# Decode-token recurrence of a hybrid decoder layer: outputs from the old states in the value stage, new states beside the FFN's second products

## What is computed

```python
z = einsum('bld,dn->bln', rmsnorm(h), w_in)          # queries, keys, values, gates, merge gates
# per head, per token:  S_t = diag(a_t) S_{t-1} + k_t^T v_t ;  o_t = q_t S_t
o_h, s_h = _gated_recurrence(q_h, k_h, i_h, log_f, s_h0)     # 8 heads, 128 x 128
o_g, s_g = _gated_recurrence(q_g, k_g, v_g, log_a, s_g0)     # 4 heads, 128 x 256
y = (rmsnorm(o) * silu(gate)) @ w_up                  # each branch
merged = sigmoid(m_h) * y_h + sigmoid(m_g) * y_g
h = h + rmsnorm(merged @ w_out)
u = square(relu(rmsnorm(h) @ w_ff1)); h = h + rmsnorm(u @ w_ff2)      # D_FF = 8192
h = h + sigmoid(h @ w_ple_gate) * (p @ w_ple)
```

## Time and profile before

| | |
|---|---|
| timed runs, median | 1670.41 us |
| profiled execution, first to last instruction | 1668.5 us |
| TensorE busy | 1661.8 us (100%) |
| VectorE busy | 1094.9 us (66%) |
| ScalarE busy | 810.8 us (49%) |
| GpSimd busy | 201.4 us (12%) |
| DMA, mean | 191 GB/s |

### The profile page before, as it was taken

The page is one execution under the profiler, slowest core; times in us unless marked ns, Lnnn a source line. Parts: engine busy times, 40 slices in busy tenths (PEclk is TensorE's granted clock), DMA queues, the critical chain, the costliest instruction groups (busy, mean ns, idle before and its releaser), DMA issues.

```text
span 1668.5 us, 36779 instructions
## 1 busy us (share of the span) xinstructions
PE 1661.8 (100%) x13676; PEld 1657.1 (99%) x13676; DVE 1094.9 (66%) x1841; ACT 810.8 (49%) x1104; POOL 201.4 (12%) x196
## 2 busy tenths in 40 slices
PE   9999999999999999999999999999999999999999
PEld 9999999999999999999999999999999999999999
DVE  7558548989988987665697445554455445555774
ACT  8574435465465556543565334443345334443452
POOL 4100001211211100025320000000000000025200
PEclk9999999999999999999999999999999999999999
DMA  9555656665665567775555555555555555555564
GB/s 277 165 187 178 221 188 204 184 210 179 199 213 186 185 216 230 228 258 176 165 183 180 186 185 170 183 185 182 171 182 181 188 180 172 182 196 176 169 192 145
DMA packets 162596, 318.73 MB, mean 191 GB/s; under 512 B 11732, under 2 KB 96468, under 8 KB 162548
## 3 DMA queue, kind: packets, MB, share of 16 engines
q1 hardware_dynamic: 160244, 315.94, 59.4%
q10 hardware_dynamic: 2304, 2.16, 0.4%
HBM read 299.97 MB, written 18.09 MB: 191 GB/s over the span
## 4 chain that ended last, share of the span: by engine, by line
PE 99%; DVE 0%; issue 0%; ACT 0%; POOL 0%; POOLq 0%
PE bank L320 28%; PE bank L321 28%; PE bank L322 28%; PE bank L338 3%; PE bank L340 3%; PE bank L343 3%; PE bank L640 2%; PE bank L653 1%; PE bank L629 1%; PE bank L671 0%; PE bank L685 0%; PE bank L679 0%; PE bank L590 0%; PE bank L651 0%; PE bank L672 0%; PE bank L610 0%
## 5 line engine op out<-in xcount | busy, mean ns | idle before, releaser
L295 ACT CAST whi<-raw 128x1024 fp32r<-128x1024 f32 x533 | 548.5, 1049 | 495.8 <-PE bank L322 392.7
L320 PE MATMUL bank<-a_hi,whi 128*128 128x264 f32 x2576 | 737.1, 286 | 0.0
L321 PE MATMUL bank<-a_lo,whi 128*128 128x264 f32 x2576 | 729.9, 283 | 0.0
L322 PE MATMUL bank<-a_hi,wlo 128*128 128x264 f32 x2576 | 729.7, 283 | 0.0
L300 DVE TENSOR_TENSOR wlo<-raw,whi 128x1024 fp32r<-128x1024 f32 x518 | 628.3, 1244 | 128.6 <-ACT whi L295 128.1
L320 PEld LDWEIGHTS bank<-a_hi,whi 128*128 128x128 f32 x2576 | 485.4, 188 | 0.5 <-issue 0.3
L321 PEld LDWEIGHTS bank<-a_lo,whi 128*128 128x128 f32 x2576 | 485.6, 189 | 0.1
L322 PEld LDWEIGHTS bank<-a_hi,wlo 128*128 128x128 f32 x2576 | 483.2, 188 | 0.0
L320 PE MATMUL bank<-b_hi,whi 128*128 128x264 f32 x1280 | 363.2, 284 | 0.0
L321 PE MATMUL bank<-b_lo,whi 128*128 128x264 f32 x1280 | 362.6, 283 | 0.0
L322 PE MATMUL bank<-b_hi,wlo 128*128 128x264 f32 x1280 | 362.4, 283 | 0.0
(11 more groups left out here) (186 smaller groups left out, 1558.1 us busy)
## 6 DMA issues: line engine op xcount, KB each, us to landing
raw<-in_stream SPq DMA_DIRECT2D x533, 512.0 KB, 4.5
m_spill<-stage SPq DMA_DIRECT2D x32, 132.0 KB, 5.1
lev<-m_spill SPq DMA_DIRECT2D x16, 264.0 KB, 3.3
S<-in_state_hgrn SPq DMA_DIRECT2D x16, 256.0 KB, 5.3
out_new_hgrn_sample<-S SPq DMA_DIRECT2D x16, 256.0 KB, 4.6
S<-in_state_gla SPq DMA_DIRECT2D x8, 512.0 KB, 8.1
out_new_gla_sample<-S SPq DMA_DIRECT2D x8, 512.0 KB, 5.5
room<-in_x SPq DMA_DIRECT2D x7, 528.0 KB, 7.7
```

Source lines behind the costliest of these rows:

```text
L295: act.copy(whi[:, s, :], raw[:, s, :]).then_inc(hi_ready, 1)
L320: pe.matmul(out, whi[:, s, w], hi[:, k0 + k, :], start=start and k == 0, stop=False)
L321: pe.matmul(out, whi[:, s, w], lo[:, k0 + k, :], start=False, stop=False)
L322: mm = pe.matmul(out, wlo[:, s, w], hi[:, k0 + k, :], start=False, stop=stop and k == HT - 1)
```

## The change

The samples leave the heads.

- **Outputs from old states.** The output is computed as (q a) S + (q k) v, with q, a, k of the sample. During the value stage SyncE loads the old states in another layout: a *unit* is one head, 16 chunks of 8 key rows by 8 samples on the partitions, 8 key rows by the value width on the free dimension (128 x 1024 for HGRN, 128 x 2048 for GLA), in a ring of four. ScalarE scales a unit by eight ACTIVATEs with a per-partition scale (`SCALED_AT`: after the spill of value tiles 1 to 8, and 9, 11, 13, 14), VectorE sums it over the 8 key rows with one reduction (`SUMMED_AT`, a tile or two later), TensorE sums over the chunks with a product with `own_sample` of width 8 (`sample_out`: HGRN after value tile 11, GLA in head 0). The factors are transposed on TensorE, stored to DRAM and loaded back in the unit's layout in eight DMAs of 32-byte runs (`load_columns`), on ScalarE's queue for q a, on SyncE's for k and a.
- **Head 0** has the rest for all heads: own products, sum of squares, roots, norm (`whole_samples`, `sum_samples`, `sample_roots`, `normed_samples`). The other heads take their columns from `so_normed`.
- **New states.** 16 units of 128 x 1024 (a GLA head is two) in a ring of three, one every three second tiles of the FFN's first three blocks: VectorE multiplies by the decay (phase 0), then adds k v in two phases of four operations of width 128 (HGRN) or two of width 256 (GLA).

```diff
+V_TILES = HH + 2 * GH
+CHUNKS = P // NS_TOK
+K_CHUNK = P // CHUNKS
+UNIT = K_CHUNK * P
+SCALED_AT = {**{1 + h: h for h in range(HH)}, 9: HH, 11: HH + 1, 13: HH + 2, 14: HH + 3}
+SUMMED_AT = {**{2 + h: h for h in range(HH)}, 10: HH, 12: HH + 1, 14: HH + 2, 15: HH + 3}
...
@@ block.scalar, value stage
         def v_tile(T, par):
             split(T + 1, 1 - par)
             spill(T, par, "v_spill", T - T_V)
+            if T == T_V:
+                act.wait_ge(qa_stored, 16)
+                load_columns(act, qa_rep, qa_d, q_landed)
+            elif T == T_V + 2:
+                act.wait_ge(s_cols_turned, 1)
+                act.copy(qk_bc[:].rearrange("c h s -> c (h s)"), DG[:, 0:HEADS * NS_TOK])
+                act.copy(s_rows[:, P:3 * P], SC[1][0:HEADS * NS_TOK, 0:2 * P]).then_inc(ka_rows_ready, 1)
...
+            u = SCALED_AT.get(T - T_V)
+            if u is not None:
+                if u == 0:
+                    act.wait_ge(q_landed, 16 * NS_TOK)
+                act.wait_ge(old_landed[u % S_RING], 16 * (u // S_RING + 1))
+                slot = old_slot(u).rearrange("p (k v) -> p k v", k=K_CHUNK)
+                for k in range(K_CHUNK):
+                    last = act.activation(slot[:, k, :], slot[:, k, :], ACT.Identity, scale=qa_rep[:, u, k:k + 1])
+                last.then_inc(units_scaled, 1)
@@ block.vector, value stage
+            dve.tensor_tensor(sample_values(n), MM[T % 2][:, NP_TOK:TOK], r_bc[:, NP_TOK:TOK], ALU.mult)
+            drain(T, T % 2, stage[:, T % 2, :]).then_inc(tiles_drained, 1)
...
+                dve.wait_ge(units_scaled, u + 1)
+                dve.tensor_reduce(partial(u), old_slot(u).rearrange("p (k v) -> p v k", k=K_CHUNK), mybir.AxisListType.X, ALU.add)
@@ block.tensor, head
             slab(0)
-            turn_s(H, D)
             turn_v(H, D)
             slab(1)
             slab(2)
             slab(3)
-            outer(H, D, 0)
-            outer(H, D, 1)
             slab(4)
             slab(5)
             scores(H, D)
             turn_kd(H)
-            sample_out(H, D, 0)
-            slab(6, midway=lambda: sample_out(H, D, 1))
+            if first:
+                turn_samples()
+            slab(6)
             prob_v(H, D)
@@ block.tensor, prob_v
             pe.wait_ge(h_sem["probs_ready"], now(H))
+            pe.wait_ge(h_sem["o_scaled"], before(H))
@@ block.vector, head
-            new_states(0)
-            new_states(1)
@@ block.vector, FFN
+        def new_state(u, phase):
...
+                kept = ka_rep[:, 1, h, k0:k0 + rows].rearrange("p (k o) -> p k o", o=1).to_broadcast([P, rows, w])
+                dve.tensor_tensor(slot, slot, kept, ALU.mult).then_inc(n_decayed, 1)
+                return
+            dve.wait_ge(n_decayed, u + 1)
+            for k in range((phase - 1) * rows // 2, phase * rows // 2):
+                last = dve.scalar_tensor_tensor(out=slot[:, k, :], in0=n_values[r][:, 0:w], scalar=ka_rep[:, 0, h, k0 + k:k0 + k + 1],
+                                                in1=slot[:, k, :], op0=ALU.mult, op1=ALU.add)
...
+            for n in range(KT):
+                T = T0 + KT + n
+                keep_t(T0 + KT, j > 0)(T, T % 2)
+                new_state(*divmod(KT * j + n, 3))
@@ load_columns
+        for s in range(NS_TOK):
+            rows = bass.AP(to.tensor, to.offset + s * pitch, [[pitch * NS_TOK, CHUNKS], [K_CHUNK, n], [1, K_CHUNK]])
+            eng.dma_start(rows, bass.AP(dram.tensor, dram.offset + s * P, [[K_CHUNK, CHUNKS], [NS_TOK * P, n], [1, K_CHUNK]]))
```

More of the change, by code:

```diff
@@ L479, in head @@
                 load_half(sp, T + 5, (T_HEADS + 5) % 2, 0, tile=T_UP, tile_half=1)
-            for r in range(2):
-                sp.wait_ge(h_sem[f"s_new{r}"], now(H))
-                sp.dma_start(new[4 * r:4 * r + 4, h].rearrange("b k v -> k b v"), S[:, r, :, 0:w])\
-                  .then_inc(s_stored[r], 16)
             if more:
@@ L684, in head_norm, with head @@
             for d in range(D):
-                mm = pe.matmul(DG[:, 0:TOK], ones[:], sq[:, d, :], start=d == 0, stop=d == D - 1)
+                mm = pe.matmul(DG[:, 0:NP_TOK], ones[:], sq[:, d, 0:NP_TOK], start=d == 0, stop=d == D - 1)
             mm.then_inc(h_sem["ss_done"], 1)
-        def head(H, D):
+        def head(H, D, first=False):
             T = 4 * H + T_HEADS
@@ L716, in norm_and_state @@
                 state(H, D)
+                if first:
+                    sum_samples()
             slab(7, midway=norm_and_state)
-        with pe.Fori(0, HH) as H:
+        with pe.Fori(0, 1) as H:
+            head(H, 1, first=True)
+        with pe.Fori(1, HH) as H:
             head(H, 1)
@@ L918, in decays @@
             act.activation(kd[:, P:NP_TOK], cum[:, P:NP_TOK], ACT.Exp, scale=-1.0).then_inc(h_sem["kd_exp"], 1)
-        for T in range(T_V, T_V + 4):
+        for T in range(T_V, T_HEADS):
             v_tile(T, T % 2)
-        decays(0)
-        tiles(act, T_V + 4, T_HEADS - 1, v_tile)
+            if T == T_V + 3:
+                decays(0)
         act.wait_ge(tiles_drained, T_V)
@@ L1001, in _ @@
         turned(0, 1)
-        with act.Fori(0, HH - 1) as H:
+        with act.Fori(0, 1) as H:
+            head(H, 1, 1, first=True)
+        with act.Fori(1, HH - 1) as H:
             head(H, 1, 1)
@@ L1117, in accumulated @@
             square_last(3, t_acc[:, KT - 1, :])
+        for r in range(N_RING):
+            act.wait_ge(n_stored[r], 16 * len(range(r, UNITS, N_RING)))
         next_input(T_GATE, 8, 3, accumulated, None, KT)
@@ new lines, in sample_values @@
+        def sample_values(n):
+            if n < HH:
+                return vs_all[:, n * NS_TOK:(n + 1) * NS_TOK]
+            return gla_by_sample(vs_all)[:, (n - HH) // 2, n % 2, :]
+        for n in range(V_TILES):
+            T = T_V + n
+            split(T + 1, 1 - T % 2)
+            dve.wait_ge(stage_stored[T % 2], 16 * (n // 2) + 16)
+            tile_done(dve, T)
+            dve.tensor_tensor(sample_values(n), MM[T % 2][:, NP_TOK:TOK], r_bc[:, NP_TOK:TOK], ALU.mult)
+            drain(T, T % 2, stage[:, T % 2, :]).then_inc(tiles_drained, 1)
+            if n == 1:
+                dve.wait_ge(h_sem["cum_ready"], now(0))
+                level_half(0)
+                level_half(1)
+            u = SUMMED_AT.get(n)
+            if u is not None:
+                dve.wait_ge(units_scaled, u + 1)
+                dve.tensor_reduce(partial(u), old_slot(u).rearrange("p (k v) -> p v k", k=K_CHUNK), mybir.AxisListType.X, ALU.add)                   .then_inc(units_summed, 1)
@@ L1290, in head @@
+        def head(H, D, more=True, opening=False):
             T = 4 * H + T_HEADS
@@ L1307, in gate_tile @@
                 last.then_inc(tiles_drained, 1)
-            def new_states(r):
-                dve.wait_ge(s_landed[r], 16 * H + 16)
-                dve.wait_ge(h_sem[f"outer{r}"], now(H))
-                for i in range(4):
-                    s, b = S[:, r, i, 0:D * P], NP_TOK + 4 * r + i
-                    last = dve.scalar_tensor_tensor(out=s, in0=s, scalar=cum[:, b:b + 1], in1=outer_at(D, r, i),
-                                                    op0=ALU.mult, op1=ALU.add)
-                last.then_inc(h_sem[f"s_new{r}"], 1)
             def level_operands(l):
@@ L1408, in _ @@
         split(T_HEADS + 1, (T_HEADS + 1) % 2)
-        with dve.Fori(0, HH) as H:
+        with dve.Fori(0, 1) as H:
+            head(H, 1, opening=True)
+        with dve.Fori(1, HH) as H:
             head(H, 1)
@@ L1674, in head @@
-            k = hk[:, H, :] if D == 1 else zk[:, H - HH, :]
-            pool.tensor_copy(k_b[:], k)
-            pool.wait_ge(v_landed, 16 * H + 16)
-            pool.wait_ge(h_sem["s_turned"], before(H))
-            for i, src in enumerate([k] + [v_st[:, d, :] for d in range(D)]):
-                to = s_feat[:, i, :].rearrange("c (g s) -> c g s", g=3)[:, :, 0:NS_TOK]
-                column = src[:, NP_TOK:TOK].rearrange("c (o b) -> c o b", o=1).to_broadcast([P, 3, NS_TOK])
-                last = pool.tensor_copy(to, column)
@@ L1683, in head @@
-            last.then_inc(h_sem["kq_ready"], 1)
-            pool.wait_ge(h_sem["s_parts_ready"], now(H))
-            pool.wait_ge(h_sem["outer1"], before(H))
-            keys = ks_tok[:].bitcast(F32).rearrange("b (o k) -> b o k", o=1).to_broadcast([S_ROWS, NS_TOK, P])
-            on_row = own_row[:].rearrange("b (c o) -> b c o", o=1).to_broadcast([S_ROWS, NS_TOK, P])
-            pool.tensor_tensor(k_diag[:], keys, on_row, ALU.mult).then_inc(h_sem["k_diag_ready"], 1)
-        with pool.Fori(0, HH) as H:
+            pool.tensor_copy(q_b[:, 0:NP_TOK], zq[:, H, 0:NP_TOK])
```

354 lines of the change are left out of this document (248 added, 106 removed).

## The result

The change makes the kernel slower. Its median is 1683.76 us (four runs, 1682.35 to 1685.59) against 1670.49 us for the kernel before on the same chip (four runs); the ratio is 1.0079, 95% interval 1.0067 to 1.0092. The forecast was 1664 us, with 1677 as the end of its range. The profiled execution spans 1680.8 us, 12.3 more than before, where the sum of the forecast had 6.3 less: it is off by 18.6 us.

A forecast was written before the change was run, and what follows sets the result against it. TensorE was taken as the bound, 99% of the last chain. Span 1668.5 - 42.1 + 5.0 + 12.8 + 18 = 1662.2 us, with 1.9 from span to timed median 1664 us; range 1651 to 1677.

The forecast's parts named there:

- Removed and added on TensorE (-42.1, +5.0): Heads lose outer products, transposes and sample_out, -42.1 us; value stage and head 0 gain transposes and products, +5.0 us.
- The wait at prob_v (+12.8): In 11 heads TensorE waits for VectorE's masks before prob_v, 1.12 us (HGRN) or 1.24 us (GLA) each, +12.8 us.
- ScalarE's loop (1.0 us over a tile): Value stage: with HGRN units scaled behind the spill, ScalarE's loop takes 6.8 us, 1.0 us over the tile.
- TensorE's 0.7: Value stage: three transposes and one product with ones added on TensorE, 0.55 us, and two switches of 0.09.
- GLA in the value stage (5.6): Value stage: scaling four GLA units on ScalarE adds 2.0 + 0.8 + 0.8 + 2.0 = 5.6 us.
- The query columns (0.5 and 0.5): Start of the value stage: eight column DMAs on ScalarE's queue 0.5 us, and the columns' landing 0.5 us.
- its bound (+5): Value stage: columns landing late, up to 9.6 us after issue against a cover of 4.6, add 5 us.
- FFN (0, bound 6): FFN's second products: new states and their loads cost 0; bound 6 us if the column load lands late.
- C: Rival: value stage becomes the bound through late columns, then the reduction; 35 us there, 1681 us; chance 0.13.
- D: Rival: the granted clock falls behind TensorE's waits, about 4 us a time, four times +16, 1680 us; chance 0.05.
- B: Rival: ScalarE's units hide in the value stage, about 6 us instead of 18; 1652 us; chance 0.2.
- part 4: Value stage: ScalarE's scaling of units, column DMAs and their landing add 18 us, bounds 8 to 30.

The follow-up runs named there:

- experiment 8: Changed kernel with GLA units loaded earlier, query columns in one transfer, key columns between wide loads, scaling behind rounding, scores and token logarithms moved earlier: 1634.27 us, ratio 0.9794.
- experiment 12: Kernel of experiment 8 with its first four units of old states loaded ahead of the value stage: 1633.61 us, ratio 0.9779.
- experiment 1: Changed kernel with three of the four GLA units of old states loaded one tile earlier: 1671.06 us, ratio 1.0004.
- experiment 2: Changed kernel with the query columns stored sample by sample and fetched in one transfer instead of eight: 1680.84 us.
- experiment 9: Changed kernel with unread products of ones filling TensorE's three deep waits of the value stage and before head 0: 1682.15 us.
- experiment 4: Changed kernel with three additions of contiguous halves in place of VectorE's reduction: 1682.15 us.
- experiment 5: Changed kernel with ScalarE scaling a unit after rounding the next tile's weights, not between spill and rounding: 1663.41 us, ratio 0.9958.
- experiment 11: Kernel of experiment 8 with additions in place of the reduction and the query columns issued ahead of the first spill: 1636.86 us, ratio 0.9793.
- experiment 10: Changed kernel with only loads mended: GLA units earlier, query columns in one transfer ahead of first spill, key columns between wide loads: 1662.69 us, ratio 0.9953.

## Why the prediction was wrong

**Removed and added on TensorE (-42.1, +5.0): right, the first some 2 us too small.** Experiment 8, with nearly all waits gone, comes out 1.1 us above their sum, experiment 12 0.4 us. From prob_v to prob_v an HGRN head takes 30.41 us before (425.53 to 455.94) and 27.43 in experiment 8, 2.98 less for 2.77; a GLA head 34.34 and 29.13, 5.21 less for 5.04. What waits are left in experiment 8 hides that.

**The wait at prob_v (+12.8): right in kind, place and size.** The forecast had TensorE go on 1.13 us after it could (423.8 to 424.93). Starts of the last matmul of the half slab and of the first of prob_v, before:
```profile
425.41 0.28 PE L322 MATMUL bank<-a_hi,wlo 128*128 128x264 f32 x1
```
(prob_v at 425.53), in the changed kernel with the next head's prob_v, and in experiment 8 two prob_v in a row:
```profile
451.09 0.28 PE L370 MATMUL bank<-a_hi,wlo 128*128 128x264 f32 x1
452.34 0.70 PE L776 MATMUL bank<-pairs,v_tok 128*128 128x256 f32 x2 [0.97 <-DVE pairs L1533]
...
481.00 0.70 PE L776 MATMUL bank<-pairs,v_tok 128*128 128x256 f32 x2 [0.97 <-DVE pairs L1533]
```
```profile
416.01 0.59 PE L783 MATMUL bank<-pairs,v_tok 128*128 128x256 f32 x2
...
443.44 0.59 PE L783 MATMUL bank<-pairs,v_tok 128*128 128x256 f32 x2
```
From 0.12 us to 1.25: 1.13 more, and prob_v itself holds its slot 0.08 longer. The row of 0.97 is smaller, since it counts from the modelled end. A head takes 28.66 us and without the wait 27.43, so the price is 1.2 us, some 13.4 in eleven heads. The margin is a half slab, as the prediction had it; moving the scores gives it back.

**ScalarE's loop (1.0 us over a tile): right.** Tiles with HGRN units come every 6.63 us for 6.8. From tile 1 to tile 9 the excess over 5.8 us is 10.0 us, forecast 12.1 with TensorE's 0.7.

**GLA in the value stage (5.6): the step that failed.** Tiles 9 to 15 took 52.8 us, 18.0 over six tiles of 5.8. The forecast had 7.4 for them (5.6, and 1.8 of sample_out). It priced ScalarE's width-256 ACTIVATEs and took the data to be there. Its only sentence on the transfers was a mean, "about 250 GB/s over the longer tile, not full". A mean share says nothing of a transfer's lateness: what counts is when it is issued, how long it takes, and when it is wanted. `LOADED_AT` could be read off the code. The entry 11 puts the load behind that of tile 11, whose slot is freed by the subtraction for tile 9, during tile 8; the unit is wanted after tile 9's drain, one tile later. From issue to want it was 7 us (221.22 to 228.3); with 6.4 us for half a megabyte a whole one was not to be expected in that. 10.6 us were lost there, and experiment 1 gave 10.4 of the span back: with its loads one tile earlier these six tiles are 8.1 over, for the 7.4 of the forecast.

**The query columns (0.5 and 0.5).** The first step between drains was 9.8 us, 4.0 over a tile. Each of the eight issues took 0.63 to 0.70 us on ScalarE's queue, where I had taken the 0.34 of a spill for a transfer of 192 runs (1,536 in all eight). I had looked for lateness in the landing, and its bound (+5) covers what experiment 2 found in the end: both ways led to the same 4 us.

**FFN (0, bound 6): the second failure, 4.6 us.** "Has about 14 us" left out what the load is queued behind: SyncE needs 10 us to issue the fourteen transfers ahead of the weight slab. Of the 4.6 us, 2.9 are the wait; behind it 16 matmuls ran at 0.22 us for 0.12 (925.00 to 928.70 us), which is the other 1.6 and a price of the lower clock.

**Not in the sum:** head 0's wait (2.1 us by its row, 2.3 from start to start), two table loads of 1.28 us each on ScalarE's path; and the lower clock at the start of head 0, 18 matmuls (279.6 to 283.6 us), 1.5 us by experiment 9.

Together: 10.6 + 3.0 (columns) - 2.1 (loop) make 11.5 of the value stage's 11.7 us; 4.6 come at FFN's loads; in the heads 2.3 + 1.5 + 0.6 (prob_v) - 2.2 (removed work) make 2.2 for the 1.9 of the table; 0.4 lie before and behind. Of the 18.6 us, 3.1 are thus the clock's, 1.5 and 1.6, each behind a wait for data that came late.

**The rivals.** C named the value stage, 35 us there, and 1681 us. Size and place were nearly those that came (32.2 and 1683.8), and of its mechanism the first half, the late columns, was worth 3 us and not 10; the reduction does take 2.0 and 3.8 us, but experiment 4 shows that the stage is not longer for it, and experiment 5 that the HGRN loop is not bound by it. A rival with the right number is not thereby the right account. D's fall of the clock happened, four times, and was paid in two of them, 3.1 us and not 16; D took each fall to be paid. B did not come: each HGRN unit cost its 0.83 us, round after round. The 0.13 for C was too little for what it stood for, data that comes late. The range ended at 1677 since each bound of part 4 was an extra on one term; none was for a resource without a term.

What stays open: what GLA's reductions cost where they lie on the chain, what the crowded DMA from 200 to 250 us still costs, and what widens the spread of the timed runs in experiments 8 and 11.

## What to carry to other kernels

When a change adds transfers, write down for each the instant of its issue (what frees the queue ahead of it), its landing, and the instant it is wanted; a mean DMA share replaces none of the three. Count the issues as work of their queue, and by their own shape. And where an engine waits for another each round, put new work behind what the other waits for: the same eight ACTIVATEs were worth nothing or 0.83 us a tile by which side of two roundings they stood on. When a forecast is worked out from start to start, measure its terms so too: a row of waits gave 10.5 us for what costs 13.4.

## What the runs showed of the hardware

- A `TENSOR_REDUCE` over the middle axis (float32, elements 512 bytes or 1 KB apart) takes 1.95 and 1.87 ns an input element (1996 ns for 1024, 3824 for 2048); a unit-stride `TENSOR_TENSOR` of 1024 elements takes 1.2 (1222 ns). Three additions did the same sum in 1.4 and 2.3 us. The Trainium skill (VectorE: DVE Perf Modes, The perf-mode tier table) puts both instructions in one tier; here the reduction is 1.6 times as long an element. Whether the stride or the instruction makes it so was not separated.
- The issue of a transfer of 192 runs of 32 bytes occupied ScalarE's queue for 0.63 to 0.70 us; of 384 such runs SyncE's for 0.62 in the median (one of the eight took 1.47, so that together they took 6.09), against 0.34 for a spill of 128 rows. All eight of ScalarE's in one piece, 128 rows of 384 bytes, took 0.44.
- In the changed kernel, behind four of the five waits of 2.8 to 4.7 us the matmuls ran at 0.22 instead of 0.12 us for 3.3 to 5.5 us (15 to 25 of them); behind the fifth (2.85 us, at 193.23) and the shorter ones they did not. With TensorE busy in three of these gaps it did not come there. In experiments 1 and 10 it did come behind the wait that was the fifth here (2.87 and 2.85 us; granted clock 0.74 from 193 to 197 us in the one, 0.66 from 189 to 194 in the other).
- With DMA 0.99 to 1.00 busy the core moved 283 to 295 GB/s (experiment 8, 160 to 250 us). A GLA unit of 1 MB took 10.9 us to land in the changed kernel, 7.8 where it was issued earlier.
